# Raw columns for the router, and the modulation's last pieces moved into the grouped attention

## The reference, cut to what matters

```
c_act = silu(c)
for i in range(2):
    mod = c_act @ ada_w[i] + ada_b[i]             # 1024 -> 6 x 1024
    sh1, sc1, g1, sh2, sc2, g2 = split(mod, 6)
    h = x * (1 + sc1) + sh1
    y = neighbourhood attention (i = 0) or grouped attention (i = 1), then @ w_o
    x = layer_norm(ALPHA * x + (1 + g1) * y, ln_g[i, 0], ln_b[i, 0])
    h = x * (1 + sc2) + sh2
    logits = h @ [w_group, w_expert] + b          # 36 columns: 4 groups, 32 experts
    y = sum over each token's two experts of gate * ((silu(h @ w_gate) * (h @ w_up)) @ w_down)
    x = layer_norm(ALPHA * x + (1 + g2) * y, ln_g[i, 1], ln_b[i, 1])
```

## Time and profile before

| | us |
|---|---|
| median of 3 runs (lowest to highest) | 1705.96 (1701.5 to 1706.75) |
| the profiled execution's own time | 1700.45 |
| its span | 1698.4 |
| PE busy, DVE busy | 1488.6, 540.1 |
| ACT busy, POOL busy | 209.9, 203.4 |
| mean granted clock of PE, as a share of full speed | 0.943 |

### The profile page before, as it was taken

One profiled execution on the slowest core, in us unless ns is written; L12 is line 12 of the kernel. 1 busy time (PEld: TensorE's weight loads), 2 busy tenths in 40 slices (PEclk: granted clock), 3 DMA queues, 4 the chain that ended last, 5 costly groups with the idle time before them and its releaser, 6 DMA issues.

```text
span 1698.4 us, 27829 instructions
## 1 busy us (share of the span) xinstructions
PE 1488.6 (88%) x12504; PEld 929.5 (55%) x12504; DVE 540.1 (32%) x1160; ACT 209.9 (12%) x581; POOL 203.4 (12%) x169
## 2 busy tenths in 40 slices
PE   6998998969899699988989986989899989988894
PEld 3455444527787665546545642575666545645651
DVE  2564555553585501110111111553411111111013
ACT  2122112202133000000000000231200000000000
POOL 3111101490055200000000000400200000000001
PEclk9999998989998799999999999979799999999998
DMA  9535664638686689999999999514399999999994
GB/s 348 198 136 186 242 233 153 204 125 295 243 278 240 257 354 379 427 426 428 426 428 426 425 426 373 194 50 174 138 387 420 426 428 426 426 427 427 426 414 167
DMA packets 96886, 534.33 MB, mean 315 GB/s; under 512 B 5088, under 2 KB 7296, under 8 KB 73200
## 3 DMA queue, kind: packets, MB, share of 16 engines
q1 hardware_dynamic: 92992, 519.40, 76.4%
q0 software_dynamic: 3760, 13.00, 2.0%
HBM read 531.32 MB, written 1.05 MB: 313 GB/s over the span
## 4 chain that ended last, share of the span: by engine, by line
PE 61%; DMA 23%; DVE 8%; issue 4%; ACT 2%; POOL 1%; SPq 1%; DVEq 0%; ACTq 0%; POOLq 0%
PE bk L410 27%; DMA AR<-in_moe_w_down 20%; PE bk L838 19%; PE bk L870 7%; PE bk L880 3%; PE bk L406 3%; DVE AR L956 3%; DMA ring<-in_ada_w 2%; DVE mpart L964 2%; ACT AR L1716 2%; PE bk L600 2%; DMA ring<-in_w_in 1%; POOL st L2040 1%; SPq L2206 1%; DVE AR L964 0%
## 5 line engine op out<-in xcount | busy, mean ns | idle before, releaser
L410 PE MATMUL bk<-ring,AR 128*128 128x512 f32 (+2 forms) x1024 | 385.4, 535 | 15.0 <-DMA ring<-in_w_in 7.9
L838 PE MATMUL bk<-ring,AR 128*32 128x128 f32 x5120 | 305.6, 409 | 1.2 <-DMA ring<-in_moe_w_gate 1.2
L410 PEld LDWEIGHTS bk<-ring,AR 128*128 128x128 f32 x1024 | 197.6, 196 | 188.3 <-issue 168.6
L838 PEld LDWEIGHTS bk<-ring,AR 128*32 128x32 f32 x5120 | 191.7, 127 | 102.2 <-DVE AR L956 6.8
L956 DVE TENSOR_TENSOR AR<-bk,AR 128x128 f32<-128x128 f32 (+2 forms) x76 | 24.8, 327 | 520.5 <-ACT AR L1716 471.9
L838 PE MATMUL bk<-AR 128*32 128x128 f32 x3072 | 185.4, 410 | 3.2 <-DMA AR<-in_moe_w_up 3.1
L1716 ACT ACTIVATE AR<-bk 128x128 f32<-128x128 f32 (+4 forms) x171 | 67.4, 411 | 960.4 <-PE bk L838 764.0
L870 PE MATMUL bk<-AR 128*32 128x512 f32 x384 | 139.8, 679 | 46.1 <-DMA AR<-in_moe_w_down 45.8
L2040 POOL TENSOR_TENSOR st<-st,half 128x1 f32<-128x1 f32 (+5 forms) x24 | 32.1, 1342 | 1160.3 <-DVE st L960 1056.0
L838 PEld LDWEIGHTS bk<-AR 128*32 128x32 f32 x3072 | 126.0, 128 | 55.2 <-DMA AR<-in_moe_w_up 5.7
L870 PE MATMUL bk<-ring,AR 128*32 128x512 f32 x640 | 139.8, 675 | 4.8 <-DMA ring<-in_moe_w_down 4.4
(11 more groups left out here) (143 smaller groups left out, 1083.8 us busy)
## 6 DMA issues: line engine op xcount, KB each, us to landing
ring<-in_moe_w_gate SPq DMA_DIRECT2D x48, 2048.0 KB, 23.6
ring<-in_moe_w_down SPq DMA_DIRECT2D x35, 2048.0 KB, 27.8
ring<-in_moe_w_up SPq DMA_DIRECT2D x32, 2048.0 KB, 20.5
AR<-in_moe_w_up SPq DMA_DIRECT2D x32, 2048.0 KB, 29.2
ring<-in_ada_w SPq DMA_DIRECT2D x24, 2048.0 KB, 11.2
AR<-in_moe_w_down SPq DMA_DIRECT2D x21, 2048.0 KB, 28.6
AR<-in_moe_w_gate SPq DMA_DIRECT2D x16, 2048.0 KB, 23.4
ring<-in_w_in SPq DMA_DIRECT2D x12, 2048.0 KB, 10.3
```

The source lines that it names most:

```text
L410: ins = eng.matmul(o, l, r, start=i == 0, stop=i == len(pairs) - 1)
L838: ins = eng.matmul(o[32 * f:32 * f + 32, 128 * m:128 * m + 128], XG[u][:, c, 32 * j:32 * j + 32], w[:, c, f::4], start=c == 0, stop=c == N ...
```

## The change

1. **Pieces.** DVE takes all 24 pieces; POOL's `ada` is gone. Pieces 13 to 19 are made in the neighbourhood attention, pieces 20 to 23 (sc2 and g2 of i = 1) in the grouped attention, which gets lists of its own (`GQA_ROUNDS`, `GQA_SIDE`). SP loads pieces 20 to 23 behind the grouped attention's weights. Every later piece of the first block's second layer stands one place earlier in the queue, because 13 and 14 are no longer among them.
2. **Router.** PE turns the raw residual (`raw_cols`), ACT and DVE scale it by the first half of `COMB`; the product comes from that, and DVE brings in the deviation and the mean behind it (`logits`: two operations of 36 columns, with the column sums `lsum` that `router_weights` and `router_sums` have made once). ACT norms x (`normed`), by a scale and a shift (`shift`).
3. **Order.** The gates' row products move from the end of the neighbourhood attention into `router`. The grouped attention's `w_o` goes tile by tile. POOL's `finish` of these two norms writes into ACC and waits for the selection; the gather waits for the normed x alone.

```
+LOADS, second layer: ... "b", "ada", "g", "ada", 0, "ada", 1, "ada"
-POOL_ADA = (13, 14, 22, 23)
-NA_ROUNDS = (("k2", "k3", "q2", "q3", "t14"), ("v00", "v10", "k4", "k5", "p04", "t15"),
-             ("v01", "v11", "k6", "k7", "p06", "t16"), ("v02", "v12", "t17"), ("v03", "v13", "t18"),
-             ("p14", "g0", "g1", "g2", "g3", "t19"), ("p16", "a00", "a01", "a02", "a03", "t22"),
-             ("o00", "o01", "t20"), ("o02", "o03", "t21"), ())
-NA_SIDE = ((), ("x14", "+", "+"), ("x15", "+", "+", "+", "+"), ("x16", "+", "+"), ("x17", "+"), ("x18", "+"),
-           ("x19", "+"), ("x22", "o00", "o01", "+"), ("x20", "o02", "o03", "s"), ("x21", "n"))
+NA_ROUNDS = (("k2", "k3", "q2", "q3"), ("v00", "v10", "k4", "k5", "p04", "t13"),
+             ("v01", "v11", "k6", "k7", "p06", "t14"), ("v02", "v12", "t15"), ("v03", "v13", "t16"),
+             ("p14", "g0", "g1", "g2", "g3", "t17"), ("p16", "l", "a00", "a01", "a02", "a03"),
+             ("o00", "o01", "t18"), ("o02", "o03", "t19"), ("c0",))
+NA_SIDE = ((), ("x13", "+", "+"), ("x14", "+", "+", "+", "+"), ("x15", "+", "+"), ("x16", "+"), ("x17", "m", "+"),
+           ("l", "+"), ("o00", "o01", "+"), ("x18", "o02", "o03", "s"), ("x19", "c0"))
+GQA_ROUNDS = ((), (), (), (), ("t20",), (), ("t21",), (), ("l",), ("t22",))
+GQA_SIDE = ((), ("+",), ("+",), ("+",), ("+",), ("x20", "+"), ("+",), ("x21", "n", "m", "+"), ("l", "+"), ("x22",))
...
+            def raw_cols(i, t):                       # PE
+                xv = X[:, t, :].rearrange("p (k c) -> p c k", c=NC)
+                pe.wait_ge(sem("raw"), 2 * i + t + 1)
+                for h in range(2):
+                    o = begin(h, "nT", 2 * i, t, h)
+                    for a in range(4):
+                        ins = turn(o[:, 128 * a:128 * a + 128], xv[:, 4 * h + a, :])
+                    end(ins, "nT", 2 * i, t, h)
...
             def neighbourhood():                      # PE
-                total(13, 5)
...
-                for f in ("h0", "h1", "h2", "h3"):
+                logits(0, 0)
+                for f in ("a10", "a11", "a12", "a13", "o10", "o11", "o12", "o13"):
                     unit(f)
-                norm_cols(0, 0)
-                for f in ("a10", "a11", "a12", "a13", "o10", "o11"):
-                    unit(f)
-                logits(0, 0)
-                for f in ("o12", "o13"):
-                    unit(f)
-                total(23, next_bank())
-                norm_cols(0, 1)
+                raw_cols(0, 1)
...
             def router(i):                            # PE
+                pe.wait_ge(*drained("adaT", 12 * i + 11))
+                gate_rows("g2", i, 1, 0, 6)
+                pe.wait_ge(sem("group"), i + 1)
+                gate_rows("g2", i, 1, 1, 7)
...
             def gather(q):                            # PE
-                        pe.wait_ge(sem("fin"), 2 * i + 1)
+                        pe.wait_ge(sem("xn"), 4 * i + 2)
...
+            def router_weights(i):                    # DVE
+                for w in range(2):
+                    v.step(tt(LTMP, wr[:, i, :, :], bcast(COMB[:, 2 * i, w, :], 2, 36), ALU.mult))
+                    ins = red(LPART[:, 36 * w:36 * w + 36], LTMP.rearrange("p c n -> p n c"), ALU.add)
+            def raw_cols(i, t):                       # DVE
+                free(tt(HT[:, 4:8, 128 * t:128 * t + 128], bank("nT", 2 * i, t, 1)[:, :].rearrange("p (c n) -> p c n", c=4),
+                        bcast(COMB[:, 2 * i, 0, 4:8], 2, 128), ALU.mult), "nT", 2 * i, t, 1)
+            def logits(i, t):                         # DVE
+                free(stt(tmp, lsum[:, 0, :], bn_a[:, t, 0:1], bank("rt", i, t)[:, 0:36], ALU.mult, ALU.add), "rt", i, t)
+                v.step(stt(R_L[:, t, :], tmp, st2[:, t:t + 1], lsum[:, 1, :], ALU.mult, ALU.add))
...
+            def normed(i, t):                         # ACT
+                s.tell(act(X[:, t, :], X[:, t, :], ACT.Identity, bias=st2[:, 52 + t:53 + t], scale=st2[:, t:t + 1]),
+                       sem("xn"), 4 * i + t + 1)
...
             def finish(k, n):                         # POOL
+                o = X if n % 2 else ACC
+                if n % 2 == 0:
+                    g.wait_ge(sem("sel"), n + 2)
...
-            ada(16)                                   # POOL
-                if n in (4, 5):
-                    ada(4)
-            ada(8)
...
+                    for n in range(20, 24):           # SP, behind the grouped attention's weights
+                        ada(n)
```

More of the change, by code:

```diff
@@ L437, in total, with router_sums @@
                 pe.wait_ge(sem("ones"), 1)
[L438 to L446, removed]
+                pe.wait_ge(sem("ada"), n + 1)
+                end(product(o[:, :], [(ones[:, :], part(n))]), "adaT", n)
+            def router_sums(i, b):
+                o = begin(b, "lsum", i)
+                pe.wait_ge(sem("ones"), 1)
+                pe.wait_ge(sem("lpart"), i + 1)
+                end(product(o[:, 0:72], [(ones[:, :], LPART)]), "lsum", i)
             def first_layer(l):
@@ L1344, in project @@
                 v.wait_ge(*drained("g1", i, 1))
-                for j in range(2):
-                    for t in range(NT):
+                extract(23)
+                for t in range(NT):
+                    for j in range(2):
                         o = slice(512 * j, 512 * j + 512)
@@ L1472, in grouped, with settle @@
                 turned(2)
-                attend("gqa", lambda: None)
+                todo = list(GQA_SIDE)
+                def settle():
+                    for f in todo.pop(0):
+                        if f == "+":
+                            ada(4)
+                        elif f == "n":
+                            norm_columns(2, 1, 3)
+                        elif f == "m":
+                            router_weights(1)
+                        elif f == "l":
+                            router_sums(1)
+                        else:
+                            extract(int(f[1:]))
+                attend("gqa", settle)
             def router(i):
                 L = R_L
-                v.wait_ge(*filled("rt", i))
-                v.wait_ge(sem("in2"), 16 * (8 + DEPTH))
-                free(tt(L, bank("rt", i)[:, 0:72].rearrange("p (t n) -> p t n", t=NT), bcast(br[:, i, :], 1, NT), ALU.add), "rt", i)
+                logits(i, 1)
                 lg = L[:, :, 0:4]
@@ L1865, in early_cols, with raw_cols @@
                             s.step(ins)
+            def raw_cols(i, t):
+                s.wait_ge(sem("comb"), 2 * i + 1)
+                s.wait_ge(*filled("nT", 2 * i, t, 0))
+                for c in range(4):
+                    ins = act(HT[:, c, 128 * t:128 * t + 128], bank("nT", 2 * i, t, 0)[:, 128 * c:128 * c + 128], ACT.Copy,
+                              scale=COMB[:, 2 * i, 0, c:c + 1])
+                    if c == 3:
+                        free(ins, "nT", 2 * i, t, 0)
+                    else:
+                        s.step(ins)
+            def normed(i, t):
+                s.wait_ge(*filled("nT", 2 * i, t, 1))
+                s.wait_ge(sem("shift"), 2 * i + t + 1)
+                s.tell(act(X[:, t, :], X[:, t, :], ACT.Identity, bias=st2[:, 52 + t:53 + t], scale=st2[:, t:t + 1]),
+                       sem("xn"), 4 * i + t + 1)
             def project(i):
@@ L1960, in router @@
             def router(i):
-                if i:
-                    for j in range(2):
-                        s.wait_ge(*filled("g2", i, j))
-                        free(act(G2[j], bank("g2", i, j)[:, :], ACT.Copy), "g2", i, j)
+                for j in range(2):
+                    s.wait_ge(*filled("g2", i, j))
+                    free(act(G2[j], bank("g2", i, j)[:, :], ACT.Copy), "g2", i, j)
                 s.chain()
```

223 lines of the change are left out of this document (125 added, 98 removed).

## The result

The changed kernel takes 1722.43 us (median, 1721.54 to 1730.36) beside 1704.66 for the kernel before (four executions of each; the table ahead of the prediction has three): a ratio of 1.0116, 95% interval 1.0081 to 1.0151. The forecast was 1721. The profiled execution is one of 1723.27 (span 1721.5); it is 22.8 above that of before, more than the medians are; its mean granted clock was 0.926, that of before 0.943, a difference of the same sign.

What follows compares the result with a forecast made beforehand. With DMA full, each experts' stage lasts 451, so the gathers' starts count: +9.8 to the first, +15.4 and -7.8 to the second, +17.4 on 1700.45, 1717.9; with 3 for the median 1721, range 1698 to 1735.

Steps and rivals of the forecast that it cites:

- (a): End of the first block: piece 12 lies there in time and POOL is idle, so the first projection comes 12.8 sooner.
- (b): Neighbourhood attention: DVE waits a whole fill more for x13 to x17, so rounds no longer overlap; +40.5.
- (c): From the neighbourhood attention's last rounds to the end of `w_o`: no POOL beside DVE, gate products gone; -7.9.
- (d): Router of i = 0, from the end of `w_o` to the gather: 12.0 instead of 22.0; -10.0.
- POOL's `finish`: Behind the selection of i = 0, meeting DVE's gates and `over`: costs 0, upper end 1.
- The experts' stages: Both stages still last 451 each, as long as the eight slots are full when the experts start.
- (e): Grouped attention: DVE gets four pieces and more, 30.4 in all, over its room; +15.4, bounds +4 and +22.
- The rival that DVE hides the four pieces: Grouped attention: DVE absorbs the pieces, so (e) is 4 and the time 1709; chance 0.13.
- The clock rival: Both attentions: gaps keep PE at 1.2 GHz, about 10 more, 1731; chance 0.16.
- (f): Router of i = 1, from the end of `w_o` to the second gather: 13.0 instead of 21.9, one turning added; -7.8.
- the catching-up case: Neighbourhood attention: same-round extracts cost only their direct stall, (b) is 18.5 and the time 1699; chance 0.11.
- that rival's 1729: Start of the experts: slots not full because the queue waits for piece 19 or 23, up to 10 more; chance 0.08.

Runs made afterwards that it cites:

- late12: Changed kernel with one wait put back: piece 12's issue waits until the first block's last output product is done; 1738.64 us, 1.0184 of the kernel before.
- side: Changed kernel with x13 to x17 and l taken out one DVE round later in the neighbourhood attention; 1670.74 us, 0.9767 of the kernel before.
- side2: Changed kernel with only x13 and x14 taken out one DVE round later in the neighbourhood attention; 1691.55 us, 0.9922 of the kernel before.
- normfirst: Changed kernel with both routers again turning the normed x, DVE adding only the bias behind the product; 1743.99 us, 1.0195 of the kernel before.
- light: Changed kernel with only two of DVE's eight steps for each of pieces 20 to 23; 1715.92 us, 1.0042 of the kernel before.
- warmatt: `side` plus constant turnings on PE, 56 ahead of the grouped projections and 8 or 24 in each attention round; 1674.49 us, 0.9824 of the kernel before.
- early: Changed kernel with pieces 20 and 21 taken by DVE ahead of the grouped attention; 1726.05 us, 1.0112 of the kernel before.
- slot: Changed kernel with piece 16 in another ring slot, so its transfer no longer waits for piece 15; 1713.0 us, 1.0022 of the kernel before.
- sideslot: `side` with piece 16 in another ring slot, so its transfer no longer waits for piece 15; 1675.7 us, 0.9833 of the kernel before.
- both: `side` with pieces 20 and 21 taken by DVE ahead of the grouped attention; 1670.44 us, 0.9797 of the kernel before.
- warmgap: `side` plus 56 unread constant turnings in PE's idle time ahead of the grouped attention's projections; 1675.36 us, 0.9851 of the kernel before.
- warmboth: `both` plus constant turnings on PE, ahead of the grouped projections and in each attention round; 1670.28 us, 0.9808 of the kernel before.

## Why the prediction was right, point by point

- **(a) End of the first block**, -12.8 by the working, -12.9 measured. Right in size, and both causes that it names are real: in `late12`, without the early transfer, 11.5 of the 12.9 are lost, and the rows of DVE put more than half of the 11.3 at the total on the steps that POOL no longer slows. The items listed come to 13.2, not 12.8.
- **(b) Rounds**, +40.5 by the working, +45.1 measured; the mechanism, turns instead of overlap, is shown by `side` and `side2`. The walk holds to within 1.5 up to group 5 (its 19.8 in round 2 is a slip for 20.8; the 80.5 it arrives at is right): scores of group 2 at 59.4 (58.7), of 3 at 105.5 (105.2), of 4 at 127.0 (125.9), of 5 at 143.7 (142.2). What is under-sized is rounds 5 and 6, 15.6 and 11.2 for 13.7 and 10.0: x17 could start 7.9 behind the scores, not 6.9, `router_weights` took 2.2 rather than 1.7 (four operations of 288 columns, 0.46 or 0.65 each), and after the wait of 5.09 PE is slow once more (2.08, 4.59), where I had charged full speed.
- **(c) To the end of `w_o`**, -7.9 and -9.5 measured; the items listed there add up to 6.3 only, so the 7.9 is not fully worked out. **(d) Router of i = 0**, -10.0 and -9.4. First gather +9.8 and +13.3: (b) missed by 4.6, and (c) and (d) took 1.0 of it back. `normfirst` shows that of (d) about 5 is the raw columns, and that without them some 8 more would go ahead of it, in (c).
- POOL's `finish` was costed at nothing with an upper end of 1. It does hold one DVE operation, `over`, 2.33 where the kernel before has 0.23, at 603.68, behind the gather's start at 601.59, and PE begins the experts on time at 609.40. The Trainium skill (SBUF — State Buffer, Who interferes with whom) has GpSimd and a VectorE operation with two SBUF inputs exclude each other; that row agrees, and the cover I named for it held.
- **The experts' stages**, 451 each, were 450.8 and 451.1. Between the first of them and the attention's first maxima 72.2 passed instead of 69.8, which my sum did not have: the 64 projection products took 30.16 for 27.7.
- **(e) Grouped attention**, +15.4 by the working, +14.1 measured. Right for its main reason, DVE over its room, as `light`, `warmatt` and the changed kernel's own 48.7 without a wait show. The split came out otherwise, and that the sum is near is luck in part: DVE's unbroken work took 48.7 for 52.6, and the 3 charged for slow first rounds did not occur (values of 2.00 and 1.97), while the last values, 3.65 and 2.45, and the waits around them made a tail of 8.0 where 2.0 was charged: 56.7 for 57.6. The 2.75 for DVE's own work in a round does not follow from the rows it names (61% of 4 is 2.4), but the 22.2 for all eight is right, for DVE was busy for 22.77 in that stage before. The rival that DVE hides the four pieces fell, +14.1 for its +4. The clock rival is real: the same instructions took 65.5 to 72.0 in different executions.
- **(f) Router of i = 1**, -7.8 and -6.2 measured: the second `logits` product went at the slow clock, 3.60 for 1.95.
- Rivals: the catching-up case fell ((b) was 45, not under 23.1). The slots were full at both starts, for the stages lasted as long as before and the DMA share during the gathers was 0.10 and 0.01 (10 over 1721 would be 1731, not that rival's 1729). The clock was lower, 0.926 for 0.943; the median did not reach the 1731 of its case, though one of the four executions took 1730.36.
- The sum was +17.4, the two profiled executions differ by 22.8, the medians by 17.8. The terms missed by -0.1 (a), +4.6 (b), -1.6 (c), +0.6 (d), -0.5 (experts), +2.4 (projections), -1.3 (e) and +1.6 (f), together +5.7. That the median is hit within 1.5 is luck in part: the profiled pair lies further apart than the medians do.

## What to carry to other kernels

When work is moved from one engine's list to another's, look first at the round in which its producer ends: where the consumer frees the producer's buffers only behind such an entry, an entry with the same round number as the fill that feeds it turns two overlapped pipelines into one that takes turns. Six of them cost 52 us here, and one place later they cost nothing. A gain of 38 us in the routers, at `w_o` and at the block's end was hidden behind this, and the kernel with the entries moved is some 2% faster than before. Relieving a bound engine can show nothing while the engine behind it loses as much to a lower clock, as in `early`, so read the granted clock of the stage together with the busy time, and do not fill a gap with work that can end after what it waits for.

## What the runs showed of the hardware that was not expected

The same grouped attention, instruction for instruction, takes 65.5 to 65.9 from the first scores to `w_o` in four profiled executions (the changed kernel, `slot`, `sideslot`, `warmgap`) and 71.9 to 72.0 in three (`late12`, `side`, `normfirst`), with a granted clock of 0.80 and 0.68; `side2` lies between, 68.9 at 0.74. The first two value products are 2.00 and 1.97 in the first group, 3.67 and 3.67 in the second, and 3.68 and 2.00 in `side2`. PE does the same work ahead of it, and only the moments differ: the projections took 30.2 to 30.3 in three of the first four, 27.7 or 29.7 in the others. In `warmgap` both were good, 27.70 and 65.9. The Trainium skill (TensorE: Matmul & The Clock Gate, Part 1) has the clock throttled by default and released by activity; the rows agree in that waits go ahead of slow products, and `warmatt` and `warmboth`, with PE kept busy, have values of 1.90 to 2.00 throughout. What decides between 65.9, 68.9 and 72.0 for one and the same list stays open.
